# Two token tiles of the output projection's first weight slice, computed inside the delta-rule stage of a hybrid decoder layer

## The reference, cut to what matters

```python
q, k, v, beta, g = (to_chunks(t) for t in (q * dk ** -0.5, k, v, beta, g))   # group A: gated delta rule
...
mixed = jnp.concatenate([oa, ob, oc], axis=-1).astype(x.dtype)               # (tokens, 1024)
o = mixed @ P['w_out'][l]                                                    # 1024 x 1024
x = x + (gate1 * rmsnorm(o, P['g_post_mix'][l])).astype(x.dtype)
h = (rmsnorm(x, P['g_pre_ffn'][l]) * (1.0 + scale2) + shift2).astype(x.dtype)
up = h @ P['w_up'][l]
```

## Time and profile before

| what | value |
|---|---|
| median of 3 runs | 1727.79 us (1727.01 to 1729.09) |
| the profiled execution, its own time | 1730.32 us |
| its span, first to last instruction | 1728.2 us |
| mean granted TensorE clock | 0.946 of full speed |
| instructions | 27692 |
| TensorE matmul busy | 1570.9 us (91%) |
| VectorE, GpSimd, ScalarE busy | 1029.7, 718.7, 622.3 us |
| delta rule's last instruction, by the trace | DVE L2088, ends 857.75 us |
| output projection's first instruction | SyncE L2179, 858.99 us |

### The profile page before, as it was taken

One profiled execution on the slowest core, in us unless ns is written; L12 is line 12 of the kernel. 1 busy time (PEld: TensorE's weight loads), 2 busy tenths in 40 slices (PEclk: granted clock), 3 DMA queues, 4 the chain that ended last, 5 costly groups with the idle time before them and its releaser, 6 DMA issues. The chain is left out here.

```text
span 1728.2 us, 27692 instructions
## 1 busy us (share of the span) xinstructions
PE 1570.9 (91%) x10611; PEld 1382.4 (80%) x10611; DVE 1029.7 (60%) x1717; ACT 622.3 (36%) x1109; POOL 718.7 (42%) x822
## 2 busy tenths in 40 slices
PE   5689989999789877999699898999999999999995
PEld 2568879999566655799577698999999999788874
DVE  1462007650266654654334598887777777769895
ACT  2432114331244443122223444333333343544352
POOL 0542013322000017785103448999999998000011
PEclk7899999999899998888799999999999999999998
DMA  8345541331311138432153111222222222986872
GB/s 325 120 132 183 174 143 55 96 92 29 119 55 59 41 105 239 108 108 76 66 166 98 61 60 69 82 76 75 76 76 75 76 78 86 308 279 195 278 245 86
DMA packets 137365, 210.45 MB, mean 122 GB/s; under 512 B 38680, under 2 KB 78920, under 8 KB 134034
## 3 DMA queue, kind: packets, MB, share of 16 engines
q1 hardware_dynamic: 130066, 198.66, 35.4%
q10 hardware_dynamic: 7168, 10.03, 1.7%
HBM read 165.60 MB, written 42.91 MB: 121 GB/s over the span
## 5 line engine op out<-in xcount | busy, mean ns | idle before, releaser
L2871 DVE SCALAR_TENSOR_TENSOR kept<-kept 128x1024 f32<-128x1024 f32 x84 | 149.6, 1781 | 60.5 <-ACT kept L2787 59.0
L3190 POOL TENSOR_SCALAR fd_ss<-fd_ss 128x1 f32<-128x1 f32 (+1 forms) x9 | 4.8, 528 | 234.3 <-ACT fd_junk L3312 234.3
L2233 PE MATMUL lane<-op_w,h_hi 128*128 128x512 f32 (+1 forms) x288 | 92.4, 402 | 9.4 <-DVE op_w L2331 8.6
L825 PE MATMUL fp_ps<-h_hi,fp_whi 128*128 128x364 f32 (+1 forms) x384 | 87.3, 336 | 8.5 <-ACT fp_whi L893 8.5
L498 PE MATMUL tp_psZ<-tp_wA,h_hi 128*128 128x512 f32 (+3 forms) x288 | 86.1, 381 | 4.1 <-POOL h_lo L420 2.4
L825 PE MATMUL fp_ps<-h_lo,fp_whi 128*128 128x364 f32 (+1 forms) x384 | 85.9, 332 | 0.0
L825 PEld LDWEIGHTS fp_ps<-h_hi,fp_whi 128*128 128x128 f32 x384 | 67.8, 193 | 9.2 <-ACT fp_whi L893 9.2
L867 POOL TENSOR_TENSOR fp_wlo<-fp_w,fp_whi 128x1024 fp32r<-128x1024 f32 x15 | 38.4, 2561 | 82.5 <-ACT fp_whi L893 82.5
L2233 PEld LDWEIGHTS lane<-op_w,h_hi 128*128 128x128 f32 (+1 forms) x288 | 52.9, 186 | 24.6 <-DVE op_w L2331 9.0
L2733 ACT ACTIVATE fu_whi<-fu_s 128x512 fp32r<-128x512 f32 x40 | 25.3, 632 | 126.2 <-PE lane L2582 83.7
L2582 PE MATMUL lane<-fu_thi,w_hi 128*128 128x272 f32 x320 | 67.0, 291 | 3.8 <-POOL w_lo L2628 3.8
(11 more groups left out here) (457 smaller groups left out, 4778.9 us busy)
## 6 DMA issues: line engine op xcount, KB each, us to landing
wa<-in_w_ada SPq DMA_DIRECT2D x24, 1024.0 KB, 5.7
w_raw<-in_w_up SPq DMA_DIRECT2D x88, 256.0 KB, 2.7
fd_b<-in_w_down SPq DMA_DIRECT2D x86, 256.0 KB, 3.8
fd_a<-scr_y SPq DMA_DIRECT2D x86, 256.0 KB, 3.9
scr_y<-kept SPq DMA_DIRECT2D x21, 544.0 KB, 4.2
fp_w<-in_w_fm SPq DMA_DIRECT2D x15, 512.0 KB, 3.6
scr_qkv<-fp_y SPq DMA_DIRECT2D x9, 512.0 KB, 3.2
dr_stg<-scr_qkv SPq DMA_DIRECT2D x8, 576.0 KB, 6.1
```

Source lines behind the costliest of these rows:

```text
L825: pe.matmul(ps[k][:, n, 0:w], w_hi[:, k, kk, :], h[:, kk, c:c + w], start=(kk == 0 and h is K.h_hi), stop=False)
L2233: last = pe.matmul(psO[t % FRONT][0:ROWS[t], c:c + 512], h[:, kk, cols(t)], wo[:, w, kk, c:c + 512], start=(kk == 0 and m == 0), stop=(kk ...
L2871: one = dve.scalar_tensor_tensor(yp, a, w, yp, ALU.mult, ALU.add)
L3190: pool.tensor_scalar(ss[0:rows, k, 1:2], ss[0:rows, k, 0:1], 1.0 / D, EPS, ALU.mult, ALU.add).then_inc(r_chain, 1)
```

## The change

Six matmuls each for two token tiles (t = 0 and 1, weight slice 0) are done in the delta rule, by TensorE, between the loop's last `turn_out(NP - 2)` and the last tile's `turn_out(NP - 1)`. For this:

- A new buffer `K.wo_first` holds the high and low part of slice 0. ACT writes the high part ahead of `values(8)` in the last turn, DVE the low part between `scaled(7)` and `state(8)`.
- SyncE loads slices 0 and 1 raw into `K.w_raw`, in its turn i = 7 behind `gates(6)` and ahead of `again(8)`. As S0 lies there, its write to `s_S` moves from behind the loop to turn i = 5, between `gates(4)` and `again(6)`; turn 7 waits for it.
- `S2`, `R` and `oq` move into `K.rows`, whose first contents are no longer read; the solver's small buffers move to the other side of SBUF, under the place of `wo_first` and of the first `w_up` parts. The PSUM lanes of the output projection are allocated ahead of the delta rule, and its banks 0 to 7 are these lanes.
- In the output projection, slice 0 is split already, and slice 1 lies raw in SBUF: ACT and DVE begin with slice 1. SyncE loads only slices 2 to 7 there, into four buffers; the first four have no wait. TensorE does slice 0 for tile 2 alone, with no wait, then slices 1 to 7 for the three tiles.

```diff
@@ delta_rule, sync
             for i in range(3, NP):
                 again(i)
                 gates(i - 1)
+                if i == 5:
+                    sp.wait_ge(s0_set, PAIRS)
+                    sp.dma_start(K.s_S, S0[:]).then_inc(s0_out, 16)
+                if i == 7:
+                    sp.wait_ge(s0_out, 16)
+                    for k in range(2):
+                        sp.dma_start(wo_raw[:, k * D:(k + 1) * D], K.w_out_d[:, k]).then_inc(K.wo_in[k], 16)
...
             gates(NP - 1)
-            sp.wait_ge(s0_set, PAIRS)
-            sp.dma_start(K.s_S, S0[:]).then_inc(s_out, 16)
             sp.wait_ge(s_set, NP)
             sp.dma_start(K.p_S, S[:]).then_inc(s_out, 16)
-            sp.wait_ge(s_out, 32)
+            sp.wait_ge(s_out, 16)
@@ delta_rule, tensor, behind the loop
+            def ahead(t):
+                c0 = t * P
+                for c in range(0, D, 512):
+                    for m, (x, w) in enumerate(((K.h_hi, 0), (K.h_hi, 1), (K.h_lo, 0))):
+                        pe.matmul(flat(K.lane[t][:])[:, c:c + 512], x[:, 0, c0:c0 + P], K.wo_first[:, w, c:c + 512], start=(m == 0), stop=False)
+
+            pe.wait_ge(K.wo_lo_set, 1)
+            pe.wait_ge(h_set, 2 * 3)
+            pe.wait_ge(tt6_set, 2 * (NP - 1))
+            ahead(0)
+            ahead(1)
             turn_out(NP - 1)
@@ delta_rule, scalar, last turn, ahead of values(i)
+                else:
+                    act.wait_ge(K.wo_in[0], 16)
+                    act.wait_ge(t_out[NG - 1], 32)
+                    act.wait_ge(t_out[NG - 2], 32)
+                    act.activation(K.wo_first[:, 0], wo_raw[:, 0:D], ACT.Copy).then_inc(K.wo_hi_set, 1)
@@ delta_rule, vector, last turn, ahead of state(i)
+                else:
+                    dve.wait_ge(K.wo_hi_set, 1)
+                    dve.tensor_tensor(K.wo_first[:, 1], wo_raw[:, 0:D], K.wo_first[:, 0], ALU.subtract).then_inc(K.wo_lo_set, 1)
@@ output_projection, sync
-            for kk in range(KD):
-                after(sp, wlo_set, kk - RAW + 1)
-                sp.dma_start(raw[:, kk % RAW], K.w_out_d[:, kk]).then_inc(raw_in[kk % RAW], 16)
+            for kk in range(2, KD):
+                if kk >= RAW + 2:
+                    sp.wait_ge(wlo_set, kk - RAW)
+                sp.dma_start(raw_of(kk), K.w_out_d[:, kk]).then_inc(raw_in[(kk - 2) % RAW], 16)
...
+            sp.wait_ge(wlo_set, 1)
             for m in range(2):
@@ output_projection, tensor
             for kk in range(KD):
-                pe.wait_ge(wlo_set, kk + 1)
-                for t in range(FRONT):
+                if kk:
+                    pe.wait_ge(wlo_set, kk)
+                for t in range(0 if kk else AHEAD, FRONT):
                     slice_of(t, kk)
@@ output_projection, scalar and vector
-            for kk in range(KD):
-                act.wait_ge(raw_in[kk % RAW], 16 * (kk // RAW + 1))
+            for kk in range(1, KD):
+                if kk == 1:
+                    act.wait_ge(K.wo_in[1], 16)
+                else:
+                    act.wait_ge(raw_in[(kk - 2) % RAW], 16 * ((kk - 2) // RAW + 1))
...
-            for kk in range(KD):
-                dve.wait_ge(whi_set, kk + 1)
+            for kk in range(1, KD):
+                dve.wait_ge(whi_set, kk)
```

More of the change, by code:

```diff
@@ L1404, in delta_rule @@
         ot = sb("dr_ot", [P, 2, H, P])
-        R = sb("dr_R", [P, H, HD])
-        oq = sb("dr_oq", [P, H, HD])
+        R, oq = (K.rows[:, n * W_A:(n + 1) * W_A].rearrange("p (h d) -> p h d", h=H) for n in range(2))
         vn = sb("dr_vn", [P, H, HD])
@@ L1412, in delta_rule @@
         S = sb("dr_S", [P, PAIRS, HD])
-        S2 = K.w_raw[:].rearrange("p a b n -> p (a b n)")[:, PAIRS * NBATCH * HD:PAIRS * (NBATCH + 1) * HD].rearrange("p (j d) -> p j d", j=PAIRS)
+        S2 = K.rows[:, 2 * W_A:2 * W_A + PAIRS * HD].rearrange("p (j d) -> p j d", j=PAIRS)
+        wo_raw = K.w_raw[:].rearrange("p a b n -> p (a b n)")
         S0 = K.w_raw[:].rearrange("p a b n -> p (a b n)")[:, 0:PAIRS * NBATCH * HD].rearrange("p (j b d) -> p j b d", j=PAIRS, b=NBATCH)
@@ L1416, in delta_rule @@
         kqT = dc[:, D_ROOM + 2 * NBATCH * HD:D_ROOM + 2 * NBATCH * HD + PAIRS * 2 * NSAMP].rearrange("p (j w t) -> p j w t", j=PAIRS, w=2)
-        bank = [own.enter_context(nc.psum_tensor(f"dr_ps{i}", [P, 512], F32)) for i in range(8)]
+        bank = [K.lane[i // 2][:, i % 2, :] for i in range(8)]
         Q = {(0, 0): bank[0], (1, 0): bank[1], (0, 1): bank[2], (1, 1): bank[3]}
@@ L1431, in delta_rule @@
                                      "o_mm s2_set s_set osb_set sq_set red_set rn_chain rn_set oo_set og_set ot_mm h_set hh_set").split())
-        sk_mm, sk_set, pick_set, st_mm, s0_scaled, s0_set, s_out = (
-            sem("dr_" + n) for n in "sk_mm sk_set pick_set st_mm s0_scaled s0_set s_out".split())
+        sk_mm, sk_set, pick_set, st_mm, s0_scaled, s0_set, s0_out, s_out = (
+            sem("dr_" + n) for n in "sk_mm sk_set pick_set st_mm s0_scaled s0_set s0_out s_out".split())
         g_in, la_out, la_in = ([sem(f"dr_{n}{k}") for k in range(3)] for n in ("g_in", "la_out", "la_in"))
@@ L2148, in output_projection @@
         raw = sb("op_raw", [P, RAW, D])
-        wo = sb("op_w", [P, 2, KD, D], F32R)
+        wo = sb("op_w", [P, 2, KD - 1, D], F32R)
+        AHEAD = 2
         hf = sb("op_h", [P, KD, P])
@@ L2170, in output_projection, with weights, raw_of @@
         block = own.enter_context(nc.Block())
+        def weights(m, kk):
+            return wo[:, m, kk - 1] if kk else K.wo_first[:, m]
+        def raw_of(kk):
+            return K.w_raw[:].rearrange("p a b n -> p (a b n)")[:, D:2 * D] if kk == 1 else raw[:, (kk - 2) % RAW]
         def cols(t):
@@ L2232, in slice_of @@
                     for m, (h, w) in enumerate(((K.h_hi, 0), (K.h_hi, 1), (K.h_lo, 0))):
-                        last = pe.matmul(psO[t % FRONT][0:ROWS[t], c:c + 512], h[:, kk, cols(t)], wo[:, w, kk, c:c + 512],
+                        last = pe.matmul(psO[t % FRONT][0:ROWS[t], c:c + 512], h[:, kk, cols(t)], weights(w, kk)[:, c:c + 512],
                                          start=(kk == 0 and m == 0), stop=(kk == KD - 1 and m == 2))
@@ L2304, in hi_up @@
                 act.activation(K.w0_hi[:, k], K.w_up_raw[:, 0, HK * k:HK * k + HK], ACT.Copy).then_inc(w0_hi_set, 1)
-            for kk in range(KD):
-                act.wait_ge(raw_in[kk % RAW], 16 * (kk // RAW + 1))
-                act.activation(wo[:, 0, kk], raw[:, kk % RAW], ACT.Copy).then_inc(whi_set, 1)
+            for kk in range(1, KD):
[3 more added lines that the diff above has]
+                    act.wait_ge(raw_in[(kk - 2) % RAW], 16 * ((kk - 2) // RAW + 1))
+                act.activation(weights(0, kk), raw_of(kk), ACT.Copy).then_inc(whi_set, 1)
             for t in range(NT):
@@ L2328, in _ @@
         def _(dve):
-            for kk in range(KD):
-                dve.wait_ge(whi_set, kk + 1)
-                dve.tensor_tensor(wo[:, 1, kk], raw[:, kk % RAW], wo[:, 0, kk], ALU.subtract).then_inc(wlo_set, 1)
+            for kk in range(1, KD):
+                dve.wait_ge(whi_set, kk)
+                dve.tensor_tensor(weights(1, kk), raw_of(kk), weights(0, kk), ALU.subtract).then_inc(wlo_set, 1)
             dve.wait_ge(g_in, 16 * (2 + NBATCH))
@@ L3552, in build @@
                     forgetting_attention(nc, ctx, K)
+                K.lane = [late.enter_context(nc.psum_tensor(f"lane{i}", [P, 2, 512], F32)) for i in range(4)]
+                K.wo_in, K.wo_hi_set, K.wo_lo_set = [sem(f"wo_in{k}") for k in range(2)], sem("wo_hi_set"), sem("wo_lo_set")
+                with ExitStack() as first:
+                    K.bm = sb(first, "dr_bm", [96, 2, 16, 16], side="right")
+                    K.bt = sb(first, "dr_bt", [96, (NT + 2) // 2, 16, 16], side="right")
+                    K.btT = sb(first, "dr_btT", [96, 2, 16, 16], side="right")
+                    K.bx = sb(first, "dr_bx", [96, 256], side="right")
+                    K.parts = sb(first, "dr_parts", [64 + 2 * H_A, TOK], BF16, "right")
+                    K.mid = sb(first, "dr_mid", [2 * H_A, 512], BF16, "right")
+                K.w0_hi, K.w0_lo = (sb(late, n, [P, 2, KD // 2, P], F32R, "right") for n in ("w0_hi", "w0_lo"))
+                K.wo_first = sb(mixer, "wo_first", [P, 2, D], F32R, "right")
                 delta_rule(nc, ctx, K)
```

9 lines of the change are left out of this document (1 added, 8 removed).

## The result

| | before | after |
|---|---|---|
| median | 1727.11 us (8 runs, 1722.89 to 1732.09) | 1715.4 us (8 runs, 1713.73 to 1719.92) |
| ratio, 95% interval | | 0.9937 (0.9919 to 0.9955) |
| profiled execution, its time and span | 1730.32, 1728.2 | 1717.47, 1715.4 |
| mean granted clock | 0.946 | 0.952 |

The kernel became faster, by 10.9 us (7.8 to 14.0) by the ratio. The sign and both places of the gain were forecast, and the question for the experiments is where the rest came from.

What follows compares the result with a forecast made beforehand. TensorE, busy 91% of the span, was taken as the bound, with time to win only in its idle or slow stretches. Gains of 8.5 + 0.5 = 9.0 us off the 1727.8 us median gave 1718.8 us, range 1717.0 to 1723.0.

Steps and rivals of the forecast that it cites:

- The sum: Whole kernel: 8.5 us from the output projection's front plus 0.5 us from the last transposes, 9.0 us gained.
- the range: Whole kernel's median: between 1717.0 and 1723.0 us, with 88% for faster, 7% for same and 5% for slower.
- Twelve matmuls in the gap: End of delta rule: they fit TensorE's wait for POOL, taking 5.1 us at no cost, and save 2.8 us later.
- The transposes: Last turn_out of the delta rule: they run at the higher clock, saving 0.5 us, bounds 0 and 0.6.
- The start at the barrier: Output projection's front: TensorE starts at once, slow for 4.2 us, no wait for slices; 8.5 us gained including the twelve's 2.8.
- The moved transfers: Sync queue, turns 5 and 7: later decay matrices by 2.6 and 3.8 us still land before their readers; cost 0.
- B: Rival at the output projection's front: clock rises after 8 us instead of 4.2, gain 6.8 us, 1721.0 us; 14%.
- C: Rival in the delta rule: moved transfers come late for POOL and the solver, up to 6.4 us, middle 1722.0 us; 10%.
- D: Rival at the delta rule's end: the twelve matmuls run behind POOL's gate, gain only 3.4 us, 1724.4 us; 9%.
- E: Rival at the output projection's front: pauses between slices keep the clock low, slower, 1743 us; 5%.
- No loss later: Stages behind the front: a shift at 900 us was taken as a shift of the end, with nothing lost.

Runs made afterwards that it cites:

- e0_null: The kernel before itself, unchanged, run as one of the kernels under test: median 1729.06 us, ratio 1.0005 against the kernel before.
- e1: The kernel before with only the new places of buffers and PSUM lanes; loads, splits and matmuls in old order: 1727.75 us, ratio 1.0000.
- e4: The changed kernel, measured again without alteration on the same chip as the other runs: median 1717.78 us, ratio 0.9946 against the kernel before.
- e5: The changed kernel plus ten extra matmuls with unused results behind the last transposes: median 1716.76 us, ratio 0.9936 against the kernel before.
- e6: The changed kernel with slice 1 also split in the last turn, twenty-four matmuls moved and slice 2 loaded ahead: 1714.35 us, 0.9921 against the kernel before.
- e8: The changed kernel, but slice 1 is loaded by the output projection instead of ahead: median 1721.98 us, ratio 0.9964 against the kernel before.
- e2_no_ahead: The changed kernel without the twelve matmuls in the delta rule; all three tiles take slice 0 in the output projection: 1722.08 us, 0.9967 against the kernel before.
- e3_moves: As e1, plus the moved transfers: s_S written in turn 5, slices 0 and 1 loaded in turn 7 but unused: 1728.38 us, 1.0001 against the kernel before.

## Why the prediction was wrong, point by point

**The sum was right.** The forecast of 9.0 us lies within both measured intervals, 10.9 (7.8 to 14.0) and 9.3 us (6.0 to 12.6), and its terms stand in the profiles: 8.08 and 7.75 us in the front (8.5 forecast), 0.46 us in the tail in the first profile (0.5 forecast). The tail moves with the clock too: from the last tile's state products to the barrier it is 20.3 to 20.9 us in the five profiles without the twelve matmuls and 19.8 in both of the changed kernel.

**The step that failed is the range**, as the prediction put it: "give or take 1.5 for where the clock rises here and at the later seams", and with it the low end of 1717.0. It gave the clock a term at this seam and behind it, and none ahead of it, and its base was the median of three runs, which lay within 2.1 us. Thirty later runs of the kernel before lay within 12.2 us (1721.14 to 1733.29), and the median of the changed kernel was 1715.4 in eight runs, below the range, and 1717.8 in seven, inside it. That difference is the luck of the draw: it is the same code, and the median of its mean granted clocks was 0.953 in the eight and 0.951 in the seven. The e0_null profile and those of e1 to e4 show a source in the delta rule's turns, from 16.2 to 19.2 us each by the clock, and a second one ahead of them. The rows for it were in the first profile, whose turns are 19.2, 17.6 and 16.2 us long over the same code. I had read the turns' timeline for its waits and not compared the turns with each other. Their sums in the seven profiles named above run from 120.7 to 126.7 us, 3 us to either side; with that added, the low end would have been about 1714 by my estimate.

**Twelve matmuls in the gap**: right. Their preparation cost nothing on the path, and they needed 3.5 us instead of 5.1, since the clock rose 0.9 us into them. I had let it rise 3.7 us after their start at the earliest, so at the batch's end. In the profiles of e4, e5, e6 and e8 it rose 1.6, 3.0, 2.5 and 4.1 us into them, so this too is drawn. The moved matmuls are worth 42.41 - 34.5 less 42.41 - 36.84, so 2.3 us in the front (2.8 forecast: the slow part of the front is longer in the changed kernel, 5.4 and 6.1 us against 4.8 in e2_no_ahead).

**The transposes**: 1.37 to 0.80 us, as forecast. The Trainium skill, "TensorE: Matmul & The Clock Gate", part 4, has it that the higher clock doesn't engage for transposes; the trace disagrees as far as their speed goes, with 0.55 us for the three where the clock was up and 0.90 in e2_no_ahead, where it was down. Whether transposes by themselves bring the clock up, no run here shows.

**The start at the barrier**: right. Matmul 0.04 us after the first transfer, no wait for any slice. The clock was low at the start, as taken, and rose 5.4 us later, not 4.2; that is 12.7 slow matmuls (5.4 / 0.427) instead of 9.8, some 0.5 us, and the front missed its forecast by 0.4. Part of this was to be seen: the clock before rose at 869.0, not at 868.6, since the window from 868 to 869 has it at 0.50 throughout, so that rise took 4.1 us and not 3.7. The Trainium skill, the same page, part 1, tells of one kernel with 6, 11 or 14 slow ones from run to run; the two profiles of the changed kernel agree in kind, with 5.4 and 6.1 us or 12.7 and 14.3 slow matmuls in the same front.

**The moved transfers**: cost 0 was right (e3_moves, 1.0001), and the price of 3.8 us was about right, with 4.4 us in one profile and about 3 in three. What was wrong was the time that it was added to: the last decay matrix of tile 8 took 6.2 us to land and not the median of 4.8, so the margin ahead of its reader was gone and not 0.8 us. POOL's next idle time took it up.

**The rivals.** B (the clock late in the front) came in part: 5.4 us for 4.2. C's lateness came, without its effect. D did not: TensorE had 2.19 us to spare. E did not: no pause stood between the slices, and the clock was up by 860.

**No loss later**: tile 3 to the end is 826.7 to 827.2 us in all profiles looked at, from 826.8 in the kernel before and 826.73 in the changed one to 827.2 in e1.

## What to carry to other kernels

A stage that begins with a load, a rounding and a subtraction has its latency on the path, even with its transfers issued first thing: preparing the first two slices in the idle time of the stage before took away 5.7 us, and twelve matmuls moved into a gap another 2 to 3. When a loop's turns have the same instructions, list their lengths: if they come in steps with the granted clock, a forecast's range must hold that draw, and a few extra matmuls where TensorE waits anyway may hold the clock. Compare segments between landmarks in two profiles, not only their ends.

## What the runs showed that I had not expected

- The clock's draw in the turns behind the first is removed by two matmuls of 512 columns per turn, at 0.1 us of cost (16.27 against 16.17 us).
- POOL's gate took 1.91 us instead of 0.99 when it ran beside DVE's subtraction of slice 0 (838.46 beside 838.30 above; 1.00 us for the gates of the turns before). It was off the path. I did not test what the two share.
- A barrier follows the last engine's work by 1.2 us, for the two engines seen: 1.24 after DVE in the changed kernel, 1.21 after TensorE in e5_warm.
